# Sparse attention of a mixer on one core: 64-row products and a softmax per item, or full 128 x 128 products and one softmax for all heads

## The reference

```python
proj = x @ w_in[l]
(h_a, b_a, c_a, uv, q, kc, vc, ksl, vsl, kw, vw, gl) = jnp.split(proj, split_points, axis=-1)
...
# 8 heads of 64 in 2 key groups of 4; nsa_attention:
kc = compress_kv(k_cmp, ck_pe, ck_w1, ck_b1, ck_w2)      # 15 compressed keys
vc = compress_kv(v_cmp, cv_pe, cv_w1, cv_b1, cv_w2)
pc = masked_softmax(sc, cmp_end[None, :] <= t[:, None])
o_cmp = jnp.einsum("bgrsn,bngd->bsgrd", pc.astype(vc.dtype), vc)
ps = masked_softmax(ss...)     # selected blocks: with 256 tokens all of them, causal
pw = masked_softmax(sw, mw)    # window of 512: causal too
g = jax.nn.sigmoid(gate_logits).reshape(bn, s, G, R, 3)
o = g[..., 0, None] * o_cmp + g[..., 1, None] * o_s + g[..., 2, None] * o_w
```

## Time and profile before

| | us |
|---|---|
| median of 3 runs | 2109.59 |
| lowest, highest | 2106.09, 2111.62 |
| profiled execution | 2107.43 |
| its span | 2105.6 |

### The profile page before, as it was taken

The page is one execution under the profiler, slowest core; times in us unless marked ns, Lnnn a source line. Parts: engine busy times, 40 slices in busy tenths (PEclk is TensorE's granted clock), DMA queues, the critical chain, the costliest instruction groups (busy, mean ns, idle before and its releaser), DMA issues.

```text
span 2105.6 us, 22900 instructions
## 1 busy us (share of the span) xinstructions
PE 2001.6 (95%) x9614; PEld 1647.3 (78%) x9614; DVE 1284.3 (61%) x1344; ACT 1016.1 (48%) x1105; POOL 134.2 (6%) x116
## 2 busy tenths in 40 slices
PE   7988999997987999997999999999999999999998
PEld 5777888877866888885888777788878878777886
DVE  3466898886666888886554534655455554446554
ACT  5545676663534776673443343444344434434442
POOL 1030000002012000001000300100010011001000
PEclk9988999998977999998999878999999999789999
DMA  8435999995423999995656521465655556116551
GB/s 277 160 121 183 337 360 320 329 348 175 140 68 123 359 337 319 354 342 189 197 179 199 174 80 41 144 216 171 191 198 181 170 163 201 60 41 219 181 170 70
DMA packets 222996, 425.64 MB, mean 202 GB/s; under 512 B 10648, under 2 KB 31392, under 8 KB 222880
## 3 DMA queue, kind: packets, MB, share of 16 engines
q1 hardware_dynamic: 217040, 405.86, 56.6%
q0 software_dynamic: 5840, 18.17, 2.8%
HBM read 422.94 MB, written 1.06 MB: 201 GB/s over the span
## 4 chain that ended last, share of the span: by engine, by line
PE 89%; DVE 6%; ACT 2%; issue 1%; POOL 1%; DMA 1%; POOLq 0%; DVEq 0%; SPq 0%; ACTq 0%
PE ps L428 25%; PE ps L430 24%; PE ps L429 24%; PE ps L2208 2%; DVE Wlo L399 2%; PE ps L511 2%; PE ps L1327 2%; ACT Whi L387 1%; PE ps L1351 1%; PE ps L2250 1%; DVE X L611 1%; PE ps L2152 1%; PE ps L2209 1%; PE ps L1188 1%; PE ps L2214 1%
## 5 line engine op out<-in xcount | busy, mean ns | idle before, releaser
L399 DVE TENSOR_TENSOR Wlo<-raw,Whi 128x2048 fp32r<-128x2048 f32 x382 | 860.9, 2256 | 627.1 <-ACT Whi L387 626.8
L387 ACT ACTIVATE Whi<-raw 128x2048 fp32r<-128x2048 f32 (+1 forms) x391 | 735.7, 1885 | 559.8 <-PE ps L430 554.8
L428 PE MATMUL ps<-Whi,XTh 128*128 128x512 f32 (+1 forms) x1856 | 719.0, 387 | 19.4 <-DVE XTl L523 17.8
L430 PE MATMUL ps<-Whi,XTl 128*128 128x512 f32 (+1 forms) x1856 | 703.8, 379 | 0.0
L429 PE MATMUL ps<-Wlo,XTh 128*128 128x512 f32 (+1 forms) x1856 | 703.3, 379 | 0.0
L428 PEld LDWEIGHTS ps<-Whi,XTh 128*128 128x128 f32 x1856 | 361.9, 195 | 92.1 <-DVE XTl L523 11.5
L429 PEld LDWEIGHTS ps<-Wlo,XTh 128*128 128x128 f32 x1856 | 362.3, 195 | 61.7 <-issue 1.7
L430 PEld LDWEIGHTS ps<-Whi,XTl 128*128 128x128 f32 x1856 | 360.2, 194 | 64.0
L428 PE MATMUL ps<-Whi,hTh 128*128 128x512 f32 x608 | 239.1, 393 | 0.0
L430 PE MATMUL ps<-Whi,hTl 128*128 128x512 f32 x608 | 236.8, 390 | 0.0
L429 PE MATMUL ps<-Wlo,hTh 128*128 128x512 f32 x608 | 236.7, 389 | 0.0
(11 more groups left out here) (294 smaller groups left out, 1433.0 us busy)
## 6 DMA issues: line engine op xcount, KB each, us to landing
raw<-in_moe_w_gate SPq DMA_DIRECT2D x64, 1024.0 KB, 7.1
raw<-in_moe_w_up SPq DMA_DIRECT2D x64, 1024.0 KB, 7.0
raw<-in_moe_w_down SPq DMA_DIRECT2D x64, 1024.0 KB, 7.4
raw<-in_ffn_gate SPq DMA_DIRECT2D x44, 1024.0 KB, 5.2
raw<-in_ffn_up SPq DMA_DIRECT2D x44, 1024.0 KB, 5.1
raw<-in_ffn_down SPq DMA_DIRECT2D x40, 1024.0 KB, 5.1
raw<-in_w_in SPq DMA_DIRECT2D x20, 1024.0 KB, 5.4
raw<-in_a_w_in SPq DMA_DIRECT2D x12, 1024.0 KB, 10.6
```

Of the source, the lines that this page charges most:

```text
L387: act.activation(Whi[:, i % NS, 0:m * n], raw[:, i % NR, 0:m * n], ACT.Copy).then_inc(w_rounded, tick(w_rounded, "rounded", i))
L399: dve.tensor_tensor(Wlo[:, i % NS, 0:m * n], raw[:, i % NR, 0:m * n], h.bitcast(f32), ALU.subtract).then_inc(w_rest, tick(w_rest, "rest", i))
L428: pe.matmul(o, xh(k, t), h[:, q, :], start=k == first, stop=False)
L430: x = pe.matmul(o, xl(k, t), h[:, q, :], start=False, stop=k == end)
```

## The change

The attention computes the same from other shapes.

- Keys are laid out as `kz`: for each group the keys of that group on its 64 partitions and zeros on the other 64 (`zeros` on DVE writes them once in a layer). One product of 128 rows gives both kinds m of a head at once (256 columns for t = 0, 512 for t = 1), and one mask product covers a whole bank. The values of four heads go through one product of 512 columns (`P` with both groups' 64 columns by `wT`); the half that belongs to the other group is not read.
- The compressed attention is done once for all heads: `scores_cmp` (8 products of 32 columns) and one softmax over 240 numbers per partition, ahead of `turn_(0)`; `flip_cmp` (2 transposes) ahead of `turn_(1)`. In `values` it is four products of 128 rows with `vcz`, which holds zeros outside the rows of its head.
- The gate columns join kw: two units of 4 x 280 in place of one of 8 x 256 and one of 8 x 24. The job gl, `gl_turn`, and the transposes of the position table (`prep`) and of the gmlp weights (`prep_gw`) go; the host lays those out, and the rows of `w_out`, instead. `q_turn` and `keys_cmp` now stand between the two units of kw, and `k_turn` right behind the second.
- `values` waits for the copies of all four heads before its first product; before, for each head before its own.

```diff
-    MIX_J = [("kv", 1792, 2304), ("q", 1280, 1792), ("kw", 2304, 2560), ("gl", 2560, 2584), ("uv", 768, 1280),
+    MIX_J = [("kv", 1792, 2304), ("q", 1280, 1792), ("kw", 2304, 2584), ("uv", 768, 1280),
...
-            plan_cols(("mx", l, n), A["w_in_2"][l], a, b)
+            plan_cols(("mx", l, n), A["w_in_2"][l], a, b, 4 if n == "kw" else None)
...
-            self.kT = area("mx_kT", [128, 2, 256])
+            self.kz = area("mx_kz", [128, 2, 2, 256])
...
-            pe.wait_ge(*on("hgs", l, 1))
-            for g in range(2):
-                x = pe.matmul(PS[b][64 * g:64 * g + 64, 0:15], M.w2[:, 0, :], M.hg[:, 0, 15 * g:15 * g + 15],
-                              start=True, stop=True)
-            x.then_inc(pe_done, tick(pe_done, "kc", l))
+            pe.wait_ge(*on("zeros", l))
+            pe.wait_ge(*on("hgs", l, 0))
+            pe.matmul(PS[b][:, 0:32], M.w2[:, 0:2, :].rearrange("p a d -> p (a d)"), M.hg[:, 0].rearrange("p g n -> p (g n)"),
+                      start=True, stop=True).then_inc(pe_done, tick(pe_done, "kc", l))
             b = bank(pe, "vc", l)
+            pe.wait_ge(*on("hgr", l))
+            pe.matmul(PS[b][:, 0:64], M.hgr[:, :, :].rearrange("p r n -> p (r n)"), M.w2[:, 2, :],
+                      start=True, stop=True).then_inc(pe_done, tick(pe_done, "vc", l))
...
+        def scores_cmp():
+            b = bank(pe, "mc", l)
+            pe.wait_ge(*on("qTs", l, 1))
+            pe.wait_ge(*on("kcs", l))
+            for t in range(2):
+                for r in range(4):
+                    x = pe.matmul(PS[b][:, 128 * t + 32 * r:128 * t + 32 * r + 32], qT[:, r, t * 128:(t + 1) * 128],
+                                  M.kcz[:, :, :].rearrange("p g n -> p (g n)"), start=True, stop=True)
+            x.then_inc(pe_done, tick(pe_done, "mc", l))
+
+        def flip_cmp():
+            b = bank(pe, "wc", l)
+            pe.wait_ge(*on("mcw", l))
+            for t in range(2):
+                x = pe.transpose(PS[b][:, t * 128:(t + 1) * 128], M.Sc[:, t].rearrange("p h n -> p (h n)"),
+                                 cst[:, C_ID:C_ID + 128])
+            x.then_inc(pe_done, tick(pe_done, "wc", l))
 
         def scores(i):
             g, t = ITEMS[i]
             kn = 128 * (t + 1)
-            ps = slice(64 * g, 64 * g + 64)
             pe.wait_ge(*on("qTs", l, 1))
             pe.wait_ge(*on("kTs", l))
+            pe.wait_ge(*on("zeros", l))
             pe.wait_ge(*on("mask"))
             for rr in heads(t):
                 b = bank(pe, "ms", l, i, rr)
-                s = PS[b][:, :].rearrange("p (r m n) -> p r m n", m=2, n=kn)
+                s = PS[b][:, :].rearrange("p (a n) -> p a n", n=kn)
                 for j, r in enumerate(rr):
-                    for m in range(2):
-                        pe.matmul(s[:, j, m, :], qT[ps, r, t * 128:(t + 1) * 128], kT[ps, m, 0:kn], start=True, stop=False)
-                        x = pe.matmul(s[:, j, m, kn - 128:kn], idr[:, :], mkr[:, :], start=False, stop=True)
+                    pe.matmul(s[:, 2 * j:2 * j + 2, :], qT[:, r, t * 128:(t + 1) * 128], kz[:, g, :, 0:kn],
+                              start=j == 0, stop=False)
+                x = pe.matmul(s[:, :, kn - 128:kn], idr[:, :], bc(mkr[:, 0:1], (0, 2 * len(rr)), (1, 128)),
+                              start=False, stop=True)
                 x.then_inc(pe_done, tick(pe_done, "ms", l, i, rr))
...
 
         def flip(i):
             g, t = ITEMS[i]
             u = i % 2
...
             nbl = 2 * (t + 1)
...
-            u = i % 2
             nbl = 2 * (t + 1)
             b = bank(pe, "mo", l, i)
+            for rr in heads(t):
+                pe.wait_ge(*on("wts", l, i, rr[0]))
+            w = M.wT[:, 0:4 * nbl, :].rearrange("p (r n) q -> p n r q", n=nbl)
+            for n in range(nbl):
+                m, k = n // (t + 1), n % (t + 1)
+                c = 2176 + 256 * m
+                pe.matmul(PS[b][:, :], P[:, k, c:c + 128], w[:, n], start=n == 0, stop=False)
+            pe.wait_ge(*on("wcs", l))
+            pe.wait_ge(*on("vcs", l))
             for r in range(4):
-                h = 4 * g + r
-                po = slice(64 * (h % 2), 64 * (h % 2) + 64)
-                o = PS[b][po, (r // 2) * 128:(r // 2) * 128 + 128]
-                pe.wait_ge(*on("wts", l, i, r))
-                for n in range(nbl):
-                    m, k = n // (t + 1), n % (t + 1)
-                    c = 2176 + 256 * m + 64 * g
-                    pe.matmul(o, P[:, k, c:c + 64], M.wT[:, r * nbl + n, :], start=n == 0, stop=False)
-                pe.wait_ge(*on("wcs", l, i))
-                x = pe.matmul(o, M.vc[0:15, g, :], M.wTc[0:15, u, r, :], start=False, stop=True)
+                x = pe.matmul(PS[b][:, r * 128:(r + 1) * 128], M.vcz[:, 2 * r + g, :],
+                              M.wcT[:, t, :], start=False, stop=r == 3)
             x.then_inc(pe_done, tick(pe_done, "mo", l, i))
...
             if z == 1:
-                prep_gw()
                 hidden_cmp()
         for z in run("kw"):
             if z == 0:
                 q_turn()
                 keys_cmp()
-        job_t_pe(pe, ("mx", l, "gl"), ready)
         k_turn()
         for z in run("uv"):
             if z == 0:
-                gl_turn()
+                scores_cmp()
                 turn_(0)
             if z == 1:
+                flip_cmp()
                 turn_(1)
...
+                if n == "kw":
+                    act.activation(M.gl[:, t, :], PS[b][:, 256:280], ACT.Sigmoid).then_inc(
+                        act_done, tick(act_done, "gl", l, t))
...
+        def exp_cmp():
+            C = M.Sc[:, :, :, 0:15]
+            act.wait_ge(*on("mcd", l))
+            act.activation(C, C, ACT.Exp).then_inc(act_done, tick(act_done, "mce", l))
+
+        def flip_cmp():
+            act.wait_ge(*on("wc", l))
+            act.activation(M.wcT[:, :, :], turned(("wc", l), 2), ACT.Copy).then_inc(act_done, tick(act_done, "wcs", l))
+            free(act_done, "wc", l)
...
+        def zeros():
+            for g in range(2):
+                dve.memset(M.kz[64 * (1 - g):64 * (1 - g) + 64, g], 0.0).then_inc(dve_done, tick(dve_done))
+            dve.memset(M.kcz[:, :, :], 0.0).then_inc(dve_done, tick(dve_done))
+            dve.memset(M.hg[:, :, :, 15:16], 0.0).then_inc(dve_done, tick(dve_done))
+            dve.memset(M.Sc[:, :, :, 15:16], 0.0).then_inc(dve_done, tick(dve_done, "zeros", l))
...
+        def keys_cmp():
+            b = where[("vc", l)]
+            dve.wait_ge(*on("vc", l))
+            dve.tensor_tensor(M.vcz[:, :, :].rearrange("p h (a d) -> p h a d", a=2), bc(PS[b][:, 0:1], (0, 8), (0, 2), (1, 64)),
+                              bc(cst[:, C_OWN:C_OWN + 1], (1, 8), (0, 2), (0, 64)), ALU.mult).then_inc(
+                dve_done, tick(dve_done, "vcs", l))
+            free(dve_done, "vc", l)
+
+        def scores_cmp():
+            C = M.Sc[:, :, :, 0:15]
+            mk = bc(cst[:, C_CADD:C_CADD + 1], (16, 2), (0, 8), (1, 15))
...
+            dve.wait_ge(*own(dve_done))
+            dve.tensor_reduce(M.cn[:, :], C, AX.X, ALU.max, negate=True).then_inc(dve_done, tick(dve_done))
+            dve.wait_ge(*own(dve_done))
+            dve.tensor_tensor(C, C, bc(M.cn[:, 0:1], (8, 2), (1, 8), (0, 15)), ALU.add).then_inc(
+                dve_done, tick(dve_done, "mcd", l))
+
+        def weights_cmp():
+            C = M.Sc[:, :, :, 0:15]
+            dve.wait_ge(*on("mce", l))
...
+            dve.tensor_tensor(C, C, bc(M.cn[:, 0:1], (8, 2), (1, 8), (0, 15)), ALU.mult).then_inc(
+                dve_done, tick(dve_done, "mcw", l))
...
+                keys_cmp()
         for z in run("uv"):
             if z == 0:
-                gl_turn()
-                turn_(0)
+                scores_cmp()
+                scores(0)
+                weights_cmp()
+                weights(0)
```

203 lines of the change are left out of this document (77 added, 126 removed).

## The result

| | before | after |
|---|---|---|
| median, us | 2108.9 (4 runs, 2106.1 to 2111.6) | 2024.8 (4 runs, 2023.2 to 2025.3) |
| profiled execution, us (its span) | 2107.4 (2105.6) | 2023.2 (2021.4) |
| mean granted clock over the span | 0.945 | 0.964 |

The ratio is 0.960, with a 95% interval of 0.958 to 0.962: the change takes 84 us, 4.0%. The forecast was 2042 us with a range of 2025 to 2076. The direction and the main mechanism stand, but the gain is 17 us larger than forecast, and the time lies just outside the range. Two terms of the sum failed: 6 us for low clock left over in the attention, where none is left, and -4.0 us for the stretch ahead of the attention, which measured -9.4.

What follows compares the result with a forecast made beforehand. PE, by its products and its clock, was taken to bound the kernel. Turns -55.9, between turns -17.7, edits outside -6.0, new waits +6, clock left over +6 gave -67.6 us: forecast 2042 us, range 2025 to 2076.

Steps and rivals of the forecast that it cites:

- the stretch ahead of the attention: Before the attention: edits there save about 3.0 us a layer, less 1 us a layer for the wait at `k_turn`.
- Clock left over: Small products (`scores_cmp`, gmlp, hidden layer) keep one low-clock stretch of 6 us in each attention: 6 us more.
- Prices at full clock: PE's float32 products of 128 rows: 0.23 us at 128 columns, 0.90 at 512; 64-row products dearer, 0.41 at 128.
- I put that down to the alternation between 64 and 128 rows: Attention scores: a 64-row product's 0.41 us against 0.23 comes from alternating row counts, so the gap goes with the change.
- The rival of the product's own price: Scores: the 64-row price is that of float32 beside the mask, not alternation; 6 us a layer, 2054 us, chance 0.07.
- The low clock follows the scores: Attention: low clock follows 64-row scores and small mask and compressed products, not values; cost some 37 us in both layers.
- the wait for `mx_P`: PE's 1.7 us wait at the windows grows by what the position table's turn filled; net effect nothing.
- New waits: PE waits 1 us each at `k_turn`, `flip(0)` and `values(3)` in turn 5: 3 us a layer, 6 us more.
- Clock as before: Rival: the attention's clock falls as often as before, 29 us in place of 6; 2065 us, chance 0.18.
- the chain in PE's place: Rival: DVE's weights and ACT's exponentials late in turns 1, 2 and 3; 13 us a layer, 2068 us, chance 0.10.
- slower: Rival: a much longer chain leaves PE idle at `flip_cmp` and `flip(i)`, turns 1 to 4; 2120 us, chance 0.04.
- no low clock left and no new wait: Rival "more": both the leftover low clock and the new waits are absent, 12 us more gain; 2030 us, chance 0.07.

Runs made afterwards that it cites:

- e_small128: Changed kernel with score products and masks in their former number and sizes, but keys zero-padded to 128 rows: 2025.6 us.
- e_rows64_grouped: Changed kernel with score products reading only their group's 64 rows, all products of an item issued before its masks: 2026.5 us.
- b_grouped: Kernel before with only the order changed: an item's 64-row score products first, then its masks, no padding: 2061.8 us, ratio 0.977.
- e_cmp4: Changed kernel with the 8 compressed score products issued four times: 2037.2 us.
- e_cmp2: Changed kernel with the 8 compressed score products issued twice: 2023.2 us.
- v_hidden: Changed kernel with the hidden layer's second half moved behind the first unit of kw, and compressed keys and values behind kw: 2016.3 us.
- v_best: Changed kernel with v_hidden's split hidden layer, and gmlp's products moved between turns 4 and 5: 2011.4 us, ratio to before 0.955.
- v_gates: Changed kernel with both sigmoids of the gates moved behind the copies of k, the two banks freed only after them: 2037.1 us.
- e_scores_old: Changed kernel with the scores alone as before (64 rows, one product per head and key set, a mask behind each): 2075.3 us.
- e_rows64: Changed kernel with score products reading only the 64 rows of their own group, same number, columns and masks: 2034.0 us.
- e_values_rows32: Changed kernel with values head by head as before, each head's compressed value product reading 32 rows instead of 128 padded: 2030.4 us.
- v_all: Changed kernel with the edits of v_hidden and v_gates, and gmlp's products moved between turns 4 and 5: 2026.5 us.

## What the prediction had right, and where it failed

Two terms failed. "Clock left over" stood at +6 us and measured 0, and the stretch ahead of the attention stood at -4.0 us and measured -9.4. They make 11.4 of the 16.6 us between -67.6 and -84.2; the turns and what lies between them make 3.0, the rest of the kernel 2.2.

**What bounds the kernel: right.** PE's work and its clock set the end before and after; DVE and ACT became no bound.

**Prices at full clock: right but for size.** A 512-column product of 128 rows was taken at 0.90 us; the four in the values of turn 5 take 3.51 us (1275.74 to 1279.25), 0.88 each. `scores_cmp` took 1.70 for 2.05. Turns 0, 2 and 3 were forecast at 4.3, 6.9 and 9.6 and took 3.97, 6.55 and 9.10; turns 1 and 4 and 5 took 5.58 and 8.92 of work for 5.3 and 9.1. 34.1 us of work for 35.2, some 2 us in both layers.

**The cause of the dear 64-row products: right.** The step "I put that down to the alternation between 64 and 128 rows" is shown by e_small128, e_rows64_grouped and b_grouped. The rival of the product's own price is refuted by 0.25 us a product in b_grouped.

**The low clock follows the scores: right as to place, incomplete as to cause.** The prediction named "64-row scores and small mask and compressed products" in one breath. The masks and the scores were dense changes of rows, and those were most of it (e_small128, b_grouped); small products of 128 rows did it in the attention only in a row of 6.8 us (e_cmp4). Whether the clock answers to the changes themselves or to the time that they stretch out is not shown.

**Clock left over, +6 us: wrong, the largest miss.** It was put there because `scores_cmp` and gmlp "are still small products". They run for 1.7 us each, and e_cmp2 shows that even twice the compressed scores leave the clock at 1.00. The third reason given, the hidden layer, could not count: it lies ahead of the attention, and its second half ran at the low clock before as well. The term is 0.

**Ahead of the attention, -4.0 us: too small, measured -9.4.** The edits themselves seem sized well (gl's 2.8 us are gone), and the new wait at `k_turn` is 1.5 us for 2. Two things were missed. First, the wait for `mx_P` was said to grow as the position table's turn no longer fills a part of it; it fell from 1.70 to 0.95 us in each layer, 1.5 us less. The step failed because it looked at PE alone. With `per=4`, kw is two units of 1120 columns instead of one of 2048 (and gl's unit is gone), so what DVE does ahead of the copy that PE waits for is shorter. DVE at that place, first in the kernel before, then in the changed one:

```profile
1185.19 4.49 DVE L399 TENSOR_TENSOR Wlo<-raw,Whi 128x2048 fp32r<-128x2048 f32 x2 [4.43 <-ACT Whi L387]
...
1184.87 3.53 DVE L401 TENSOR_TENSOR Wlo<-raw,Whi 128x2048 fp32r<-128x2048 f32 x2 [4.37 <-ACT Whi L389]
1188.31 0.75 DVE L2504 COPY mx_P<-mx_P 128x512 f32<-128x512 f32 x2
...
1190.36 1.29 DVE L401 TENSOR_TENSOR Wlo<-raw,Whi 128x1120 fp32r<-128x1120 f32 x1
```

The two subtractions ahead of the copy took 4.49 us before, both of 2048 columns; now they take 3.53, since the second has 1120 (the row merges both), as has the one of 1.29 us. Second, the clock there: 0.93 and 0.90 instead of 0.85 and 0.93. By the loss that b_grouped's clock was reckoned with, that is 8.5 + 3.5 us before and 3.4 + 4.9 after, an estimate of 3.7 us less. Over the 24 stretches with the changed code the mean is 48.9 us, over the four with the code of before 54.3: 5.4 us a layer and not 2; but the four of before spread from 50.3 to 56.6. In layer 0 of the kernel before the clock also falls right behind the wait of 1.70 us, which ends at 1190.08:

```profile
1193.00:1195.00 2.00, 2.00 (x6) 1.53 (x5) 1.23 (x4) 0.00 (x0) 0.00 (x0) 0.50 1.01 378
```

Over all runs the clock falls there in three of the four stretches with a wait of 1.70 us (both of b_grouped; layer 1 of the kernel before had no such fall) and in none of the 32 with 0.95 us. So the fall goes with the old code at this place. Whether the longer wait brings it or the turn of the position table, two records of 16 rows right ahead of the wait, no run takes apart. The later fall belongs to the hidden layer (v_hidden).

**New waits, +6 us: right.** 0.8 for 1 at `k_turn`, 0.4 for 1 at the first flip, 1.6 for 1 before the last values: 5.6 us in both layers. For the first flip some luck was in it: the steps listed for DVE add up to some 9.6 us with 0.2 for each tiny one, not to 10.3. The flip came 10.2 us after the turn's start all the same, because DVE also waited 0.6 us for ACT, which the list has not. In v_best the first and the last of the waits are gone.

**The rest of the kernel: -2.2 us,** which no term foresaw and no edit explains; executions of one kernel differ by as much.

**The rivals.** Clock as before, the chain in PE's place, slower and same are all out. The nearest was the last, "no low clock left and no new wait", at 2030 us: its first half came true in the attention. The range was too narrow at its low end: 2025 stood only 5 us below that rival, which leaves the stretch ahead of the attention as forecast but for the wait at `k_turn`, and that stretch alone missed by 5.4. That 2024.8 lies outside 2025 by 0.2 us, and not inside, is chance; the four runs spread over 2 us.

**By parts.** The new scores give 50 us, nearly all by padding the keys (in the kernel before, issuing products and masks in groups without padding gave 46); the padded compressed values give 7 to 9; values of four heads at once nothing. The 26.5 us that are left belong to one compressed softmax for all heads, to gl and to the other edits together, and were not taken apart.

## What to carry to other kernels

Where products of few rows alternate with products of 128 rows, group them by rows or pad them before anything else is rebuilt: one reordered loop gave 46 of the 84 us. Break a long row of small products with large ones that have to run anyway: that gave 8.5 us here. A bank of PSUM is free only after its last reader, so a reader moved later on ACT can stop a product that seems to have nothing to do with it: 4.1 us a layer in v_gates.

## What was not expected of the hardware

- A change between 64 and 128 rows costs 0.34 to 0.39 us there and back, from 32 to 128 rows 0.29 us; PE counts as busy meanwhile (73 of 73 us, 96 of 96 us).
- Dense changes of rows lower the granted clock although PE is never idle: 0.82 and 0.84 in the attention with 32 pairs a layer in the scores (e_scores_old), 0.97 and 1.00 with 12 (e_rows64), 1.00 with 4 (e_rows64_grouped). The 16 pairs of e_values_rows32, farther apart, left it at 1.00. Why b_grouped, with 8 pairs around the scores and 16 in the values, still has 0.95 is open.
- A row of products with 30 or 32 moving columns can lower it as well: 6.8 us of 32 columns did (e_cmp4), 3.4 us did not (e_cmp2); the hidden layer's 7 us of 30 columns did in all 30 mixers, halves of 3.5 us in two of six.
- It fell behind idle time too: behind 4.1 and 4.6 us in all four mixers of v_gates and v_all, to 0.50.
- Products with 64 weight columns and 128 moving columns leave it at 1.00, and eight items of them cost PE only 2 us more in both layers than 128 columns by 512.
